# A one-core hybrid layer: another order of the attention tiles, five of six top-k masks built inside the steps, two banks for the last output tile

## What is computed

```
h = rmsnorm(x, norm_g) * (1 + scale) + shift          # shift, scale, gate = silu(c) @ ada_w + ada_b
xr, gr, q, k, v, ga, qi, ki, wi = split(h @ w_in)
y_r = rg_lru(conv4(xr)) * silu(gr)                     # recurrent half, 512 channels
score = sum over 8 index heads of relu(qi . ki) * wi, causal
idx   = top 256 keys of score, for each query
y_a   = softmax over idx of (q . k / 8) @ v, 8 heads of 64, one shared k and v;  y_a *= silu(ga)
x = x + gate * (concat(y_r, y_a) @ w_out)
out = rmsnorm(x, final_g)
```

## Time and profile before

| | |
|---|---|
| median of 3 runs | 606.87 us (605.71 to 607.12) |
| profiled execution | 603.09 us, its span 601.3 us |
| busy in the span | PE 531.6 us (88%), DVE 429.7 (71%), ACT 384.9 (64%), POOL 211.3 (35%) |
| granted PE clock, mean | 0.949 of full |
| the chain that ended last | PE 69%, DVE 14%, ACT 7% |

### The profile page before, as it was taken

How to read it: one execution, slowest core, us unless ns; L and a number is a source line. 1 busy time by engine, 2 the same in 40 slices (tenths; PEclk the granted TensorE clock), 3 DMA queues, 4 the chain that set the end, 5 groups by cost and what they waited for, 6 DMA issues and landing times.

```text
span 601.3 us, 8070 instructions
## 1 busy us (share of the span) xinstructions
PE 531.6 (88%) x2676; PEld 441.5 (73%) x2676; DVE 429.7 (71%) x990; ACT 384.9 (64%) x683; POOL 211.3 (35%) x186
## 2 busy tenths in 40 slices
...
GB/s 301 396 348 77 74 293 101 23 106 35 37 35 36 37 67 38 36 106 106 131 152 35 136 144 0 92 14 2 71 1 70 1 71 1 70 1 71 1 70 71
DMA packets 19658, 51.98 MB, mean 86 GB/s; under 512 B 4128, under 2 KB 5152, under 8 KB 19616
## 3 DMA queue, kind: packets, MB, share of 16 engines
...
## 4 chain that ended last, share of the span: by engine, by line
PE 69%; DVE 14%; ACT 7%; issue 5%; POOL 2%; DMA 2%; SPq 1%; DVEq 0%; POOLq 0%; ACTq 0%
PE pair L1496 26%; PE pair L1621 13%; PE pair L1643 6%; PE pair L1656 5%; PE pair L1465 4%; PE pair L1599 2%; PE pair L1573 2%; PE pair L1600 2%; PE pair L1665 2%; DVE score_sb L1325 2%; DVE rank L1254 2%; PE pair L1564 1%; PE pair L1565 1%; PE pair L1442 1%; DMA x_sb<-in_x 1%
## 5 line engine op out<-in xcount | busy, mean ns | idle before, releaser
L1404 DVE TENSOR_TENSOR pt_lo<-pair,pt_hi 128x512 fp32r<-128x512 f32 (+3 forms) x96 | 50.5, 554 | 71.7 <-ACT pt_hi L1043 71.2
L1496 PE MATMUL pair<-h_hi,w_hi 128*128 128x512 f32 x304 | 98.3, 405 | 0.0
L938 ACT ACTIVATE bias_sb<-score_sb,tinies 128x1024 bf16<-128x1024 f32 (+2 forms) x93 | 95.7, 1031 | 3.2 <-DVE tinies L1207 3.1
L1496 PE MATMUL pair<-h_lo,w_hi 128*128 128x512 f32 x304 | 94.4, 392 | 0.0
L1496 PE MATMUL pair<-h_hi,w_lo 128*128 128x512 f32 x304 | 93.7, 389 | 0.0
L1193 DVE TENSOR_SCALAR_CACHE_REDUCE bias_sb<-score_sb,tinies 128x640 bf16<-128x640 f32 (+2 forms) x93 | 72.4, 801 | 0.8
L746 POOL TENSOR_SCALAR w_hi<-w_raw 128x1024 fp32r<-128x1024 f32 (+1 forms) x22 | 23.6, 1075 | 135.0 <-DMA w_raw<-in_w_tiles 115.3
L1496 PEld LDWEIGHTS pair<-h_hi,w_hi 128*128 128x128 f32 x304 | 56.5, 189 | 14.5 <-issue 4.5
L1496 PEld LDWEIGHTS pair<-h_lo,w_hi 128*128 128x128 f32 x304 | 57.4, 189 | 12.4
L1496 PEld LDWEIGHTS pair<-h_hi,w_lo 128*128 128x128 f32 x304 | 57.3, 188 | 12.2
L1043 ACT ACTIVATE pt_hi<-pair 128x512 fp32r<-128x512 f32 (+3 forms) x96 | 43.5, 488 | 25.8 <-PE pair L1656 23.4
...
## 6 DMA issues: line engine op xcount, KB each, us to landing
...
```

The costliest lines, as they stand in the source:

```text
L938: nc.scalar.activation(junk[i], score_sb[:, SCORE_OFF[i]:SCORE_OFF[i] + keys_of(i)], ACT.Sign, bias=cand[:, c:c + 1], scale=-1.0, accum_ou ...
L1404: nc.vector.tensor_tensor(pt_lo[:, 4 * b:4 * b + nc4, hh, :], psum[use % 2][:, 0:nc4 * P].rearrange("p (c q) -> p c q", q=P), f32(pt_hi[:, ...
L1496: ins = nc.tensor.matmul(psum[banks[half]][0:width, :], w[b][:, k, 0:width], hh[:, k, half * HALF:(half + 1) * HALF], start=(k == 0 and p ...
```

## The change

- **Order of the tiles**: `ATT` becomes [4, 3, 2, 1, 0, 7, 6, 5].
- **Ahead of the steps** stands one mask, tile 4's. The planner loses `post` and `mask` and keeps `own_thr` and the three narrow comparisons; ahead of the first comparison ACT does an Exp of one column (`warm`).
- **Inside the steps**, on DVE: a mask is cut into `ranks` (compare with 0, scan) and `biases` (the rest). Tile 3's stand in steps 1 and 2, tile 2's in 9 and 11, tile 7's in 16 and 17, tile 6's in 18 and 19, tile 5's in 20 and 21. `settle` is cut too: the small operations in step 4, the wide tiles' counts in step 6. On ACT the wide comparisons stand in steps 8, 9 and 10, and the first two high halves of yr in 11 (was 16).
- **w_out and pieces**: the high half of w_out is made in steps 2 to 9 (was 10 to 17). `OUT_START` is 14 (was 20), so one step has two pieces, and then there is one per step as before.
- **The last tile**: its halves go to banks 4 and 5, free by then, and its pieces come in the order 0, 1, 4, 5, 2, 3, 6, 7.
- **Memory and waits that follow**: two probability buffers instead of three, the ranks of the wide tiles in the place of tile 7's scores, the squares' output in `yg`, the gate's product waits for the squares and no longer for the residual sum; SP's residual loads wait for three masks instead of six.

The core of the diff:

```diff
-ATT = [1, 0, 4, 7, 6, 5, 3, 2]
+ATT = [4, 3, 2, 1, 0, 7, 6, 5]
-MASK_AT = {4 * c + 1: c for c in range(ACT_COLS)}
-WO_START = 10
-OUT_START = 20
+MASK_ORDER = (3, 4, 5, 0, 1, 2)
+RANK_AT = {1: 4, 9: 5, 16: 0, 18: 1, 20: 2}
+BIAS_AT = {2: 4, 11: 5, 17: 0, 19: 1, 21: 2}
+SETTLE_AT = (4, 6)
+CMP_AT = {8: 0, 9: 1, 10: 2}
+YR_AT = 11
+ZERO_AT = 12
+WO_START = 2
+OUT_START = 14
...
+PIECES.update({LAST_STEP - 8 + n: [56 + o] for n, o in enumerate((0, 1, 4, 5, 2, 3, 6, 7))})
...
         def prob_of(g):
-            return (prob[0], prob[1], prob_late if g >= 16 else prob_early)[g % 3]
+            return prob[g % 2]
+
+        def out_bank(ti, half):
+            return bank(3) if ti < NT - 1 else bank(4 + half)
...
-            sp.wait_ge(bias_ok, len(PICK))
+            sp.wait_ge(bias_ok, len(PICK) - ACT_COLS)
...
-            sp.wait_ge(att_ps, 16)
+            sp.wait_ge(att_ps, 8)
...
                 if o[0] == "cmp":
-                    if c < ACT_COLS:
-                        act.wait_ge(thr_ok, 2)
-                    else:
+                    if o[1] == MASK_ORDER[0]:
+                        nc.scalar.activation(warm[:, :], ones[:, :], ACT.Exp)
                         act.wait_ge(own_thr_ok, 1)
+                    compare(o[1])
...
-                if g == OUT_START - 4:
-                    act.wait_ge(bias_ok, len(PICK))
+                if g == YR_AT:
+                    act.wait_ge(bias_ok, 1)
+                    act.wait_ge(compared, len(PICK))
                     yr_half(0)
                     yr_half(1)
...
+                if g in CMP_AT:
+                    act.wait_ge(thr_ok, 2)
+                    compare(CMP_AT[g])
...
-                    nc.scalar.activation(sq_junk, x_res[ti % 2][:, half * HALF:(half + 1) * HALF], ACT.Square,
+                    nc.scalar.activation(yg[half], xs, ACT.Square,
...
+            dve.wait_ge(evac_done, len(EVAC))
+            link(nc.vector.memset(zeros[0], 0.0))
+            ranks(MASK_ORDER[0])
+            biases(MASK_ORDER[0])
             dve.wait_ge(bias01_ok, 2)
...
-                    if g == 16:
-                        dve.wait_ge(bias_ok, len(PICK))
+                    if i in PICK and g % 8 == 0:
+                        dve.wait_ge(bias_ok, MASK_ORDER.index(PICK.index(i)) + 1)
...
-                if g in MASK_AT:
-                    mask(MASK_AT[g])
+                if g == SETTLE_AT[0]:
+                    settle()
+                if g == SETTLE_AT[1]:
+                    settle_counts()
+                if g == ZERO_AT:
+                    link(nc.vector.memset(zeros[1], 0.0))
+                if g in RANK_AT:
+                    ranks(RANK_AT[g])
+                if g in BIAS_AT:
+                    biases(BIAS_AT[g])
...
-                        dve.wait_ge(x1_ok, 2 * (ti - 1) + half + 1)
-                    nc.vector.tensor_tensor(yg[half], bank(3).rearrange("p (c q) -> p c q", q=P),
+                        dve.wait_ge(sq1_ok, 2 * (ti - 1) + half + 1)
+                    nc.vector.tensor_tensor(yg[half], out_bank(ti, half).rearrange("p (c q) -> p c q", q=P),
...
                     if piece % 4 == 0:
-                        if 2 * ti + half:
+                        if ti == NT - 1:
+                            pe.wait_ge(att_min, 64)
+                        elif 2 * ti + half:
                             pe.wait_ge(y_ok, 2 * ti + half)
```

More of the change, by code:

```diff
@@ L249, in stages @@
         add("DVE", ("own", it), OWN_US, 5, (("count", it, 2), 0.1))
-    add("DVE", ("post",), 5.0, 4, *[("update", SEARCH_BITS - 1, c) for c in range(ACT_COLS)])
-    add("DVE", ("own_thr",), 0.3, 4, ("own", SEARCH_BITS - 1))
-    before = []
-    for c in MASK_ORDER:
-        n = keys_of(PICK[c])
-        add("ACT", ("cmp", c), 0.5 + n / 1200, 5, ("post",) if c < ACT_COLS else ("own_thr",), *[("cmp", b) for b in before])
-        if c >= ACT_COLS:
-            add("DVE", ("mask", c), 1.0 + n / 280, 7, ("cmp", c), *[("mask", b) for b in before])
-        before = [c]
+    add("DVE", ("own_thr",), 0.3, 0, ("own", SEARCH_BITS - 1))
+    for n, c in enumerate(MASK_ORDER[:ACT_COLS]):
+        add("ACT", ("cmp", c), 0.5 + keys_of(PICK[c]) / 1200, 5, ("own_thr",), *[("cmp", b) for b in MASK_ORDER[:n]])
     free = dict(FIRST_US)
@@ L405, in layer_kernel @@
         for i in range(2, NT):
-            tie[i] = sb(f"tie{i}", R_S + 4 * SCORE_OFF[i], [P, keys_of(i)], BF16)
-            rank[i] = sb(f"rank{i}", R_S + 4 * SCORE_OFF[i] + 2 * keys_of(i), [P, keys_of(i)], F16)
+            at = R_S + 4 * SCORE_OFF[i if i in PICK[ACT_COLS:] else PICK[0]]
+            tie[i] = sb(f"tie{i}", at, [P, keys_of(i)], BF16)
+            rank[i] = sb(f"rank{i}", at + 2 * keys_of(i), [P, keys_of(i)], F16)
         R_B = region(2 * sum(keys_of(i) for i in range(NT)))
@@ L451, in layer_kernel @@
         q_free = sb("q_free", R_Q, [P, NH, S])
-        fg_bc = q_free[:, :, 0:P]
-        yg = [q_free[:, 4 * n:4 * n + 4, P:2 * P] for n in range(2)]
+        fg_bc = q_free[:, :, ATT[0] * P:ATT[0] * P + P]
+        yg = [q_free[:, 4 * n:4 * n + 4, ATT[1] * P:ATT[1] * P + P] for n in range(2)]
         ident = sb("ident", region(512), [P, P])
@@ L493, in layer_kernel @@
         proj_ps = ((0, 1), (2, 3), (4, 5))
-        zero_ps = psum[7][:, HALF - 1:HALF]
+        zeros = [psum[b][:, HALF - 1:HALF] for b in (3, 5)]
         own_miss = psum[7][:, 0:len(PICK) - ACT_COLS].bitcast(I32)
-        low, carry = (psum[7][:, ACT_COLS * n:ACT_COLS * (n + 1)].bitcast(I32) for n in (2, 3))
+        low, carry = (psum[3][:, ACT_COLS * n:ACT_COLS * (n + 1)].bitcast(I32) for n in (2, 3))
         small_in = sem("small_in")
@@ L939, in search, with compare @@
                                      bias=cand[:, c:c + 1], scale=-1.0, accum_out=cnt[:, c:c + 1]).then_inc(count_a, 1)
+            def compare(c):
+                i = PICK[c]
+                n = keys_of(i)
+                t = bias_sb[:, BIAS_OFF[i]:BIAS_OFF[i] + n]
+                nc.scalar.activation(t, score_sb[:, SCORE_OFF[i]:SCORE_OFF[i] + n], ACT.Sign, bias=neg_thr[:, c:c + 1],
+                                     scale=sign[:, c:c + 1], accum_out=cnt[:, c:c + 1]).then_inc(compared, 1)
             relus = 0
@@ L1245, in settle, with ranks @@
                 nc.vector.scalar_tensor_tensor(neg_thr[:, act_cols], cand[:, act_cols], -1.0, sign[:, act_cols], ALU.mult, ALU.mult).then_inc(thr_ok, 1)
-            def mask(c):
+            def ranks(c):
                 i = PICK[c]
@@ L1251, in mask, with biases @@
                 t = bias_sb[:, BIAS_OFF[i]:BIAS_OFF[i] + n]
+                zero = zeros[0] if c >= ACT_COLS else zeros[1]
                 dve.wait_ge(compared, MASK_ORDER.index(c) + 1)
+                if c < ACT_COLS:
+                    dve.wait_ge(bias_ok, MASK_ORDER.index(c))
                 link(nc.vector.tensor_scalar(tie[i][:, :], t, 0.0, None, ALU.is_equal))
-                link(nc.vector.tensor_tensor_scan(rank[i][:, :], tie[i][:, :], zero_ps.to_broadcast([P, n]), float(n - 2 * TOPK), ALU.add, ALU.add))
+                link(nc.vector.tensor_tensor_scan(rank[i][:, :], tie[i][:, :], zero.to_broadcast([P, n]), float(n - 2 * TOPK), ALU.add, ALU.add))
+            def biases(c):
+                i = PICK[c]
+                n = keys_of(i)
+                t = bias_sb[:, BIAS_OFF[i]:BIAS_OFF[i] + n]
                 link(nc.vector.tensor_scalar(cols(c, nK), rank[i][:, n - 1:n], cols(c, cnt), 0.5, ALU.subtract, ALU.mult))
@@ L1307, in _ @@
                     own_threshold()
-                if o[0] == "post":
-                    settle()
-                if o[0] == "mask":
-                    mask(o[1])
                 if o[0] == "sum":
```

31 lines of the change are left out of this document (15 added, 16 removed).

## The result

| | before | changed |
|---|---|---|
| median | 606.29 us (603.57 to 607.12, 4 runs) | 612.47 us (611.55 to 615.18, 4 runs) |
| profiled execution | 603.09 us, span 601.3 | 611.87 us, span 610.1 |
| granted PE clock, mean | 0.949 | 0.957 |

The ratio is 1.0117, with a 95% interval of 1.007 to 1.0164: slower, by 4 to 10 us. The forecast was 601.9, its range 594.5 to 609. One against the changed kernel is uncertain by some 3 us either way, 2.8 of them from that kernel's own four runs; so effects of 5 us and more are clear, and smaller ones are only as good as the traces beside them.

What follows compares the result with a forecast made beforehand. Bound by PE work at full clock from 403.0 to 570.5 us, half-clock and idle PE before. Step 64's start 566.6 + tail 22.4 + end 7.3 = 596.3 us span, 601.9 as median; range 594.5 to 609.

Steps and rivals of the forecast that it cites:

- min(0): Start of step 0's minimum on DVE (step: one head of one query tile); forecast at 346.1 us, 6.6 earlier.
- min(14) past 400: Sign against the forecast: step 14's minimum on DVE starting after 400 us, where 394.1 was forecast.
- steps 0 to 13: 48.0: Time from step 0's to step 14's minimum on DVE, before output pieces: 36.5 plus clock, DVE and ACT additions, 48.0 us.
- the base of 36.5: Steps 0 to 13 without additions: eight tile-4 steps at 2.76 us, 22.1, plus tile 3 at 2.4 a step, 14.4.
- DVE: counts of the wide tiles at step 6, +3: Counts, 4.2 us with small ones, before step 5's low half on DVE; partly in idle time, +3 us, bounds 0 and 4.2.
- settling fits: 0: Step 4's settling on DVE, 1.3 us, fits into DVE's idle time and costs 0; with narrow mask parts, otherwise +4.
- +4: Low PE clock at first, rising at step 3 or 4: +4 us, ends +1 and +20.7.
- The rival with a lasting low clock: PE clock stays low to step 13: 20.7 us instead of 4, net +12, span 608, time 614; chance 0.09.
- +5.5: Masks 0, 1, 2 on DVE in steps 16 to 21: even steps leave 4.4 us; +5.5, bounds 0 and 12.7.
- tiles 7, 6, 5, 97.4: Steps of tiles 7, 6, 5 after tile 0: the earlier 101.5 us less three output pieces, 97.4 us.
- The tail: Step 64 to the end: 23.5 becomes 22.4 us, waits gone but last tile +1.1; then 7.3 unchanged.
- The full-price rival: DVE's inserted masks, counts and settling cost full length: +10 us, time 612, chance 0.08; halfway 607, chance 0.13.

Runs made afterwards that it cites:

- the last combination: Changed kernel with settling behind step 0's minimum, counts spread, masks and wide comparisons moved, w_out halves from step 4: 0.9829 to the kernel before, 593.55 us.
- shift: Changed kernel with only the wide masks' DVE parts later, ranks at steps 17, 21, 25 and biases at 18, 22, 26: ratio 0.9969 to the kernel before.
- its control: Changed kernel with only settling scratch and scan zeros moved from PSUM to SBUF: ratio 1.0183; with unread products on TensorE added, 1.007.
- the part alone: Kernel before with only the last tile's out halves in banks 4 and 5 and its new piece order: ratio 0.9953, 602.59 us.

## Why the prediction was wrong

**Right**: min(0), 346.1 against 347.1, of which 0.85 us comes from ahead of the change (ga's last evacuation starts at 340.07, not 339.22, and anywhere up to 342.6 in the other profiles); the first transpose (348, was 349.1); clock full by 360; steps 14, 15 and tiles 1 and 0 within 1 us; 7.3 us behind the last piece; no wait of the PE in the last eight pieces. min(14) past 400 was named as what would make it wrong: it is 404.95.

**Wrong, steps 0 to 13: 48.0, was 57.8.** That the last combination takes 47.4 does not confirm the base of 36.5 with its inserts: it comes to 26.8 in steps 0 to 7, where the forecast's terms make 29.1 (22.1 + 4 + 3), and to 20.5 in steps 8 to 13, where they make 18.9 (14.4 + 2.5 + 2); two misses nearly cancel. The step that failed first is "DVE: counts of the wide tiles at step 6, +3", with "settling fits: 0". From min(6) to min(7) it took 7.4 us, and from min(4) to min(5) 5.0. The sum lacked two mechanisms, the hold by POOL (1.7 and 1.5 us, and 1.1 more in step 11, all on the path) and the clock. In steps 8 to 13, 5.4 us over, the hold in step 11 is one part and the clock another: the same program took 21.1 us there in *shift*'s profile, instead of 24.3. The rest isn't divided. One row of DVE's timeline before did show the first, ya_lo beside POOL's wo_lo of 380.68 to 383.04, where six of its other seven instances take 0.69 (the seventh, at 401.07 beside POOL's yr_lo, takes 1.20):

```profile
382.32 1.26 DVE L1396 TENSOR_TENSOR ya_lo<-ya_raw,ya_hi 128x512 fp32r<-128x512 f32 x1 [0.69 <-ACT ya_hi L1027]
```

I had written "in the shadow of these steps" of POOL's eight subtractions, and they were moved into just the steps that got the settling.

**Wrong, the clock: "+4" was for a clock that rises once.** I asked when it rises and never whether it falls again in a wait that my own sum puts there. Measured with its control, whose first wait is longer (5.81 us for 3.16), that is 6.8 us, and the profiles have it in steps 4 to 24. The rival with a lasting low clock had the right place and the wrong form: the clock was full in between. The rule it leaned on, that transposes don't engage full clock (the Trainium skill, TensorE: Matmul & The Clock Gate, section Part 4: PE-mode transpose), did not decide here: tile 4's steps, of whose some 16 instructions 5 are transposes, brought it to 1.00 from 356 to 360. Nor was the PE "four fifths busy" in the 36 us at 0.50 of the kernel before: 26.3 of 35.8 us are 73%.

**Wrong, the masks in 16 to 21: "+5.5" in all, "0.5 more each" for the product with the gate behind a rank.** Steps 16 to 24 took 31.9 instead of 27.0. The even/odd reasoning had the right direction (some 2.9 us by the runs, 4.4 in the forecast). But y behind the rank was priced as its own 0.69 us, when the wait is the rank's 2.3 us: 2.34 and 1.91 us, and the clock fell behind both.

**Too dear: tiles 7, 6, 5, 97.4, was 93.5.** The base came from steps that began behind tile 4; now they begin behind tile 0, whose products still due are a fifth. That wasn't tried by itself.

**The tail**: 29.7, was 31.0, while the part alone brings 2.8 us where tile 2 is last. If the gain is the same 2.8 us in the changed kernel, the tile that now stands last costs some 3 us, not the forecast's 1.1; that wasn't run.

The full-price rival named the right time (612) by another way, and by luck: its sum has 2 us for the settling and the narrow masks, where its own list has 4, which gives 614. And DVE's operations as such are not the price: the three counts spread are 6.2 us cheaper, and the last combination, with the same operations, is 17 us faster.
